# One layer of a decoder trunk: the S5 stage rewritten in chunks of 16 with one scan in a turning frame, and parameters and bias rows worked out during the projection

## The reference, cut to what matters

```python
h = rms_norm(x, g_mix); proj = h @ w_in          # (2048,1024) @ (1024,7168)
# columns: q,k,v of 3 groups x 8 heads x 64 | u: 512 channels of S5 | gate_a | gate_b
logits = einsum('nbqhd,nbkhd->nbhqk', qb, kc) + bias    # window of 128 steps, dilation 1, 4, 16
bias = bias_table[bucket]                               # by distance, per head
# S5, per group of 16 channels (32 groups), 64 complex states:
a_bar = exp(lam * dt); b_bar = ((a_bar - 1) / lam) * b_mat
# x_t = a_bar x_{t-1} + b_bar u_t ;  y_t = Re(C x_t) + D u_t   (associative scan over 2048 steps)
y_s = gelu(y)                                           # then a sigmoid gate
x = x + (sigmoid(gate_a) * (A @ W_a) + sigmoid(gate_b) * (S @ W_s)) @ w_out
x = x + moe(rms_norm(x))                                # top 4 of 32 experts
```

## Time and profile before

| | us |
|---|---|
| three runs | 5672.62, 5674.24, 5676.24 (median 5674.24) |
| the profiled execution | 5676.82 |
| its span | 5675.2 |

### The profile page before, as it was taken

The page is one execution under the profiler, slowest core; times in us unless marked ns, Lnnn a source line. Parts: engine busy times, 40 slices in busy tenths (PEclk is TensorE's granted clock), DMA queues, the critical chain, the costliest instruction groups (busy, mean ns, idle before and its releaser), DMA issues.

```text
span 5675.2 us, 81720 instructions
## 1 busy us (share of the span) xinstructions
PE 5272.8 (93%) x30128; PEld 4680.6 (82%) x30128; DVE 3105.4 (55%) x5828; ACT 1728.8 (30%) x2756; POOL 987.1 (17%) x829
## 2 busy tenths in 40 slices
PE   8999999986996997869699999999999999999997
PEld 7888888876884886758599899899989999999997
DVE  4313130006664666625455666666677777777776
ACT  4112111110102664113232333333333344444343
POOL 0000000003310200212312231313132222222221
PEclk9999999995557998989799999999999999999999
DMA  3122221210003434434345454545456666666665
GB/s 138 67 76 72 72 76 67 78 72 5 0 0 119 142 125 146 157 137 135 115 171 170 149 185 151 191 149 190 154 191 221 212 218 220 221 219 218 219 219 186
DMA packets 237535, 802.38 MB, mean 141 GB/s; under 512 B 32503, under 2 KB 52623, under 8 KB 201521
## 3 DMA queue, kind: packets, MB, share of 16 engines
q1 hardware_dynamic: 198960, 673.21, 32.1%
q0 software_dynamic: 32656, 106.62, 7.9%
q10 hardware_dynamic: 5760, 20.45, 1.1%
HBM read 652.88 MB, written 147.89 MB: 141 GB/s over the span
## 4 chain that ended last, share of the span: by engine, by line
PE 44%; DVE 4%; ACT 1%; issue 1%; DMA 0%; POOL 0%; DVEq 0%; ACTq 0%; POOLq 0%
PE ex_g L1892 27%; PE ex_d L1906 15%; DVE ex_y L2041 2%; PE ex_g L1878 1%; ACT ex_wgh L1945 1%; DVE ex_wdl L1999 1%; DVE ex_wgl L1993 1%; DVE ex_t L2020 0%; DVE ex_bgu L2014 0%; DMA ex_xg<-h_d,ex_nxt 0%; POOL ex_y L1848 0%; DMA ex_nxt<-slots_d 0%; ACT ex_xh L1958 0%; POOL out L1851 0%; DVEq L2052 0%
## 5 line engine op out<-in xcount | busy, mean ns | idle before, releaser
L1892 PE MATMUL ex_g<-ex_xh,ex_wgh 128*128 128x256 f32 (+2 forms) x4352 | 1292.3, 297 | 71.9 <-DVE ex_t L2020 64.5
L1892 PE MATMUL ex_g<-ex_xh,ex_wgl 128*128 128x256 f32 (+2 forms) x4352 | 1284.3, 295 | 0.0
L1892 PE MATMUL ex_g<-ex_xl,ex_wgh 128*128 128x256 f32 (+2 forms) x4352 | 1284.2, 295 | 0.0
L1892 PEld LDWEIGHTS ex_g<-ex_xh,ex_wgh 128*128 128x128 f32 x4352 | 823.4, 189 | 101.6 <-issue 71.1
L1892 PEld LDWEIGHTS ex_g<-ex_xl,ex_wgh 128*128 128x128 f32 x4352 | 823.8, 189 | 8.5
L1892 PEld LDWEIGHTS ex_g<-ex_xh,ex_wgl 128*128 128x128 f32 x4352 | 824.6, 189 | 0.0
L1993 DVE TENSOR_TENSOR ex_wgl<-ex_wg,ex_wgh 128x2048 fp32r<-128x2048 f32 x274 | 626.6, 2287 | 54.8 <-ACT ex_wgh L1945 52.2
L1945 ACT ACTIVATE ex_wgh<-ex_wg 128x2048 fp32r<-128x2048 f32 x274 | 524.4, 1914 | 394.2 <-PE ex_g L1892 366.8
L1848 POOL TENSOR_SCALAR ex_y<-ex_y,ex_cur 128x1024 f32<-128x1024 f32 x82 | 294.9, 3597 | 1601.2 <-DVE ex_y L2041 1601.2
L1906 PE MATMUL ex_d<-ex_wdh,ex_ath 128*128 128x512 f32 x1312 | 523.4, 399 | 0.0
L1906 PE MATMUL ex_d<-ex_wdl,ex_ath 128*128 128x512 f32 x1312 | 515.7, 393 | 0.0
(11 more groups left out here) (354 smaller groups left out, 8656.8 us busy)
## 6 DMA issues: line engine op xcount, KB each, us to landing
ex_wg<-in_w_gu SPq DMA_DIRECT2D x276, 1024.0 KB, 5.6
ex_wd<-in_w_down SPq DMA_DIRECT2D x276, 512.0 KB, 6.3
qkv_d<-prj_o SPq DMA_DIRECT2D x144, 256.0 KB
att_blk<-qkv_d SPq DMA_DIRECT2D x48, 768.0 KB, 4.2
prj_raw<-in_w_in SPq DMA_DIRECT2D x112, 256.0 KB, 3.6
ex_bd<-in_b_down SPq DMA_DIRECT2D x34, 512.0 KB
gate_d<-prj_o SPq DMA_DIRECT2D x64, 256.0 KB
mix_ring<-gate_d SPq DMA_DIRECT2D x32, 512.0 KB, 3.8
```

The lines of the kernel that those rows point to most:

```text
L1892: last = pe.matmul(gu[j][:, 0:size], w[:, k, j, :], x[:, k, 0:size], start=(k == 0 and x is xh and w is h), stop=(k == KD - 1 and w is l))
```

## The change

**S5.** Chunks of 16, so 128 of them; four batches of four pairs (`BP`, `NB`). POOL orders a batch's tokens in one copy (128x2048) and makes `inm` of a batch in six products of 128x1024, with one buffer for all batches; the output maps are now DVE's (`output_map`, six of 128x1088). PE makes only the first 16 rows of each Toeplitz matrix (`first_rows`, two products); SP copies them shifted, by 16 transfers per batch inside SBUF (`shift`). The chunk states are multiplied by a table of cosines and sines, so that the recurrence has a real factor, scanned for the whole batch by one `tensor_tensor_scan` of 128x1024, and turned back.

**Projection.** The parameters (`maps`, at m = 3) and the tables (`table`, at m = 6, stored to DRAM) are worked out on DVE, the bias rows at m = 9 (three products on PE after tile 8); at m = 10 SP writes the bias rows 128 times over to DRAM (`rep_d`), from where attention reads them already shifted and in order. `RAW` falls to 4, `RING` to 9, and seven of the eight splits of a matrix stand at t = 15.

**Attention.** `bias_tables` and `jflip` are gone; SP loads the bias per group (`load_bias`); q of the next block is turned and saved at j = 0 and not at j = 1.

The diff, cut:

```diff
-TS = 8
+TS = 16
...
-    XR, RAW, RING, OR, OB = 3, 6, 10, 3, 6
+    XR, RAW, RING, OR, OB = 3, 4, 9, 3, 6
+    MAPS, TABLES, BIAS = 3, 6, 9
...
-            return [first] if t == 5 else [first + 1] if t == 8 else list(range(first + 2, first + KD)) if t == NT - 1 else []
+            return [first] if t == 5 else list(range(first + 1, first + KD)) if t == NT - 1 else []
...
+                        if (m, t) == (BIAS, 11):
+                            store_rows()
+                        if (m, t) == (BIAS + 1, 4):
+                            sp.wait_ge(rows_out, 16 * NG)
+                            sp.dma_start(rep_d, on_rows(rows_d.rearrange("h s -> (h s)"), P)).then_inc(rep_out, 16)
...
+                        if (m, t) == (BIAS, 8):
+                            pe.wait_ge(negated, 1)
+                            for g in range(NG):
+                                if g == 2:
+                                    pe.wait_ge(rows_saved, 1)
+                                pe.matmul(pt[g % 2][0:HG, 0:STEPS_W], rel[:, g * HG:(g + 1) * HG], hot[g], start=True,
+                                          stop=True).then_inc(rows_mm, 1)
...
+                def shift(b):
+                    sp.wait_ge(d_added, b + 1)
+                    sp.wait_ge(zeroed, 1)
+                    if b >= 2:
+                        sp.wait_ge(y_mm, BP * (b - 1))
+                    for h in range(2):
+                        for j in range(JT):
+                            sp.dma_start(intra[b % 2][SC * j:SC * (j + 1), :, h, SC * j:W],
+                                         first[SC * h:SC * (h + 1), :, 0:W - SC * j]).then_inc(f_out[b % 2], 16)
+                for b in range(NB):
+                    shift(b)
+                    if b >= 2:
+                        sp.wait_ge(o_saved, 4 * (b - 1))
+                        sp.dma_start(y_out[:, b - 2, :], yT[b % 2][:, :]).then_inc(y_stored[b % 2], 16)
+                    if b + 2 < NB:
+                        load_table(b + 2)
...
+                def input_map(b):
+                    go(outer(pool, itmp[0], rr, br, b, TS))
+                    if b:
+                        pool.wait_ge(in_turned, BP * b)
+                    outer(pool, itmp[1], ri, bi, b, TS).then_inc(inm_ready, 1)
+                    pool.wait_ge(inm_ready, 3 * b + 1)
+                    go(pool.tensor_tensor(inm[:, :, 0, :], itmp[0][:, :, :], itmp[1][:, :, :], ALU.subtract))
+                    go(outer(pool, itmp[0], rr, bi, b, TS))
+                    outer(pool, itmp[1], ri, br, b, TS).then_inc(inm_ready, 1)
+                    pool.wait_ge(inm_ready, 3 * b + 2)
+                    pool.tensor_tensor(inm[:, :, 1, :], itmp[0][:, :, :], itmp[1][:, :, :], ALU.add).then_inc(inm_ready, 1)
+                    pool.wait_ge(inm_ready, 3 * b + 3)
...
+                        last = pe.matmul(ps_f[:, q % 2, :], bblk[:, p, r, :], cpad[b % 2][:, q, r, 0:W], start=(r == 0),
+                                         stop=(r == 1))
...
+                            for k in range(KT):
+                                last = pe.matmul(ps_x[q // 2][rows, q % 2, r, :], inT[p % 2][:, k, r, rows],
+                                                 u8[b % 2][:, q, h, k, :], start=(k == 0), stop=(k == KT - 1))
...
+                def outputs(b):
+                    pe.wait_ge(f_out[b % 2], 16 * 2 * JT * (b // 2 + 1))
+                    for q in range(BP):
+                            pe.matmul(out[:, h, :], u8[b % 2][:, q, h, 0, :], intra[b % 2][:, q, h, :], start=(h == 0),
+                                      stop=False)
+                            pe.matmul(out[:, h, JT * SC:], u8[b % 2][:, q, h, 1, :], intra[b % 2][:, q, h, 0:W - JT * SC],
+                                      start=False, stop=False)
+                        if q == 0:
+                            pe.wait_ge(st_ready, b + 1)
+                        for h in range(2):
+                                last = pe.matmul(ps_y[p % 2][:, h, :], st[b % 2][:, h, r, q, :],
+                                                 cpad[b % 2][:, q, r, SC:], start=False,
+                                                 stop=(h == 1 and r == 1))
+                        last.then_inc(y_mm, 1)
...
+                def output_map(b):
+                    z = b % 2
+                    if b >= 2:
+                        dve.wait_ge(y_mm, BP * (b - 1))
+                    n = W + SC
+                    outer(dve, ctmp[0], pr, cr, b, TS + 1)
+                    go(outer(dve, ctmp[1], pi, ci, b, TS + 1))
+                    go(tt(cpad[z][:, :, 0, :], ctmp[0][:, :, :], ctmp[1][:, :, :], ALU.subtract))
+                    outer(dve, ctmp[0], pi, cr, b, TS + 1)
+                    go(outer(dve, ctmp[1], pr, ci, b, TS + 1))
+                    stt(cpad[z][:, :, 1, :], ctmp[0][:, :, :], -1.0, ctmp[1][:, :, :], ALU.mult, ALU.subtract).then_inc(
+                        cpad_ready, 1)
+                    dve.wait_ge(cpad_ready, b + 1)
...
+                        dve.memset(decay[:, :, :, 0:1], 0.0)
+                    dve.wait_ge(tab_in[z], 16 * (b // 2) + 16)
+                    dve.wait_ge(x_saved, 2 * b + 2)
+                    re, im = xs[:, :, 0, :], xs[:, :, 1, :]
+                    for t, x, w in ((rt[0], re, ct), (rt[1], im, sn), (rt[2], im, ct), (rt[3], re, sn)):
+                        tt(t, x, w, ALU.mult).then_inc(rotated, 1)
+                    dve.wait_ge(rotated, 4 * b + 4)
+                    tt(z_in[:, 0, :, :], rt[0], rt[1], ALU.add)
+                    go(tt(z_in[:, 1, :, :], rt[2], rt[3], ALU.subtract))
+                    dve.tensor_tensor_scan(flat(z_out), flat(decay), flat(z_in), 0.0, ALU.mult, ALU.add).then_inc(scanned, 1)
+                    dve.wait_ge(scanned, b + 1)
+                    re, im = z_out[:, 0, :, :], z_out[:, 1, :, :]
...
+                    for n in range(4):
+                        dve.wait_ge(o_turned, 4 * b + n + 1)
+                        dve.tensor_copy(yT[b % 2][:, :].rearrange("p (n j) -> p j n", j=TS)[:, 4 * n:4 * n + 4, :],
+                                        ps_o[:, :, :]).then_inc(o_saved, 1)
...
+                def load_bias(g):
+                    heads = slice(g * HG, (g + 1) * HG)
+                    shifted = bass.AP(rep_d.tensor, rep_d.offset + g * HG * STEPS_W + P - 1,
+                                      [[len(GROUPS) * HG * STEPS_W - 1, P], [STEPS_W, HG], [1, 2 * P]])
+                    sp.dma_start(bias[:, heads, :], shifted).then_inc(bias_in[g], 16)
...
-                        if j == 1:
+                        if j == 0:
                             turn_q(n + 1)
+                    if j == 0 and blocks[n][0] != blocks[n - 1][0]:
+                        dve.wait_ge(bias_in[blocks[n][0]], 16)
```

More of the change, by code:

```diff
@@ L607, in _ @@
[L607 to L623 removed]
+                            rows = slice(SN * h, SN * (h + 1))
@@ new lines, in chunk_states, with forward @@
+                            for k in range(KT):
+                                last = pe.matmul(ps_x[q // 2][rows, q % 2, r, :], inT[p % 2][:, k, r, rows],
+                                                 u8[b % 2][:, q, h, k, :], start=(k == 0), stop=(k == KT - 1))
+                    last.then_inc(x_mm, 1)
+                def forward(b):
+                    for q in range(BP):
+                        p = b * BP + q
+                        turn_inputs(p)
+                        turn_map(p)
+                        first_rows(p)
+                        chunk_states(p)
@@ new lines, in turn_outputs @@
+                def turn_outputs(b):
+                    pe.wait_ge(y_saved, BP * b + BP)
+                    for n in range(4):
+                        if b or n:
+                            pe.wait_ge(o_saved, 4 * b + n)
+                        for j in range(4):
+                            last = pe.transpose(ps_o[:, j, :], tok[:, 4 * n + j, b * P:(b + 1) * P], ident[:, :])
+                        last.then_inc(o_turned, 1)
+                forward(0)
+                forward(1)
+                for b in range(NB):
+                    outputs(b)
+                    if b:
+                        turn_outputs(b - 1)
+                    if b + 2 < NB:
+                        forward(b + 2)
@@ L775, in bucket_onehot @@
+                dve.wait_ge(c_in, 48)
+                dve.wait_ge(eye_ready, 1)
+                output_map(0)
+                output_map(1)
+                for b in range(2):
+                    add_skip(b)
+                    scan(b)
+                for b in range(NB):
+                    if b + 2 < NB:
+                        output_map(b + 2)
+                        add_skip(b + 2)
+                        scan(b + 2)
+                    save_yT(b)
 def bucket_onehot():
@@ L847, in attention @@
-def attention(nc, qkv_d, q_gain, k_gain, bias, ident, pieces, att_d):
+def attention(nc, qkv_d, q_gain, k_gain, rep_d, ident, pieces, att_d):
     NB, PR = 6, 3
```

762 lines of the change are left out of this document (410 added, 352 removed).

## The result

The changed kernel took 5355.22 us (median of 4 runs, 5353.55 to 5358.59) and the one before 5675.24 (4 runs), a ratio of 0.9437 (95% interval 0.9421 to 0.9453). 5369 was predicted, with 5315 to 5462.

| stretch | before | after | difference | predicted |
|---|---|---|---|---|
| until S5's block begins | 1262.3 | 1269.85 | +7.5 | +7.4 |
| S5's block to attention's first instruction (before: with the bias block) | 514.0 | 216.0 | −298.0 | −295 |
| attention, to the first product of the mixing | 438.7 | 409.0 | −29.7 | −18 |
| the rest | 3460.2 | 3458.4 | −1.8 | 0 |

The account below looks back on a forecast made before the run. PE was taken to bound the projection, and S5 at half clock. S5 −295, attention −18 and projection +7.4 sum to −305.6 on 5676.8, giving 5371.2; that execution being 2.6 above the median, 5369 us, range 5315 to 5462.

Parts of the forecast that it names:

- scan(1): S5: DVE's scan of batch 1, put at 15 us beside POOL, ending 93 us after the block's start.
- The chain itself: S5: POOL, PE and DVE work in turn, block 219 us instead of 514.0, 295 us gained.
- the rival that had a chance of 0.13: S5: DVE and POOL shut each other out, overlapping maps and scans run one after the other; 5403, chance 0.13.
- The forward parts: S5: PE's transposes, first rows and chunk states of a batch; 15.6 us for four pairs, plus restart or table switch.
- the switch of table: S5: ACT's switch of table from GELU to copy, 1.3 us, charged in forward(2), forward(3) and outputs(2).
- a restart at half clock: S5: each restart of PE's list runs at most 3 us at half clock, then at full clock.
- The turning: S5: PE turns outputs and DVE copies them, alternating on one PSUM tile; 6.4 us per batch, 12.8 for batches 2 and 3.
- The scan instruction: S5: DVE's single scan instruction for a batch, taken as 1.8 us, bounded by 1.285 and twice that.
- Shifts: S5: 16 small transfers per batch, about 6 us with issues, hidden under the 13 us scan on DVE.
- Attention: Attention: −20 for q turned one step earlier (bounds −37 and 0), +2 for group 0's bias load; sum −18 us.
- Projection: Projection: bias rows +2.4, start +2, changes of matrix +3, parameters and tables hidden; sum +7.4 us.
- the low-clock rival: S5: PE's clock stays at 1.2 GHz, +85 us after taking off 12 for restarts already counted; 5454, chance 0.17.

Follow-up runs that it names:

- pool_halves: The changed kernel with each of POOL's products of 1024 columns cut in two of 512; 5356.76 us, ratio 0.9447.
- kept_busy: The changed kernel with turns of the identity on PE in the places where it waits in S5; 5349.72 us, ratio 0.9427.
- maps_early: The changed kernel with a second PSUM tile for turned outputs and POOL's input maps made in the projection, loaded by S5 from DRAM; 5307.31 us, ratio 0.9352.
- order_back: The changed kernel with q of the next attention block turned and saved at j = 1 again; 5383.56 us, ratio 0.9492.
- order_alone: The kernel before with only q of the next attention block turned and saved at j = 0; 5645.94 us, ratio 0.9951.

## Why the prediction was right, and where its parts were not

The removal of PE's long list was right, and so was the order of the new chain; that the sum came so near is in part luck, as the table shows. The time of each point on the chain, counted from the block's start:

| end of | predicted | measured |
|---|---|---|
| POOL's map 0 | 28 | 23.3 |
| forward(0) | 47 | 40.4 |
| forward(1) | 77.6 | 64.2 |
| scan(1) | 93 | 89.1 |
| output_map(2) | 101.5 | 96.9 |
| forward(2) | 118.4 | 111.0 |
| scan(2) | 133.4 | 131.2 |
| output_map(3) | 148.1 | 147.1 |
| forward(3) | 165 | 160.1 |
| outputs(3) | 199.1 | 191.9 |
| last turning | 211.9 | 208.8 |
| block | 219 | 216.0 |

Step by step, those that took longer than predicted (scan(1) 9.5 us, scan(2) 5.2, the last turning 4.1, the turning of batch 0 with output_map(3) 1.2) make 20 us, those that took less 23. Neither alone would have left the range: without the ones the time would have been some 5335, without the others some 5378 (estimates from these rows).

- **The chain itself was right**: from batch 1 on, POOL's map, forward parts, scans and output maps followed one another as predicted, with PE waiting where it was said to (15.5 and 7.1 us for output maps 2 and 3, where some 8 each was said). What was not foreseen is that forward(0) waited 2.7 us for DVE's first output map, which took 15.2 us beside POOL and not 8.2.
- **DVE beside POOL was undersized, POOL oversized.** From the small instructions of before I read factors, 1.2 and 1.46. They need not have been factors: POOL's instructions of S5 were 0.2 to 0.75 us long there, so that a wait for a whole one was short; no run tests this on the old stage, but it fits. With 1.9 us each, DVE's 0.6 became 2.4. The scans of batches 0, 1 and 2 took 27.6, 21 and 20.4 us, not 15. It was the mechanism of the rival that had a chance of 0.13, yet at the time of the forecast and not at that rival's 5403; this is the luck in it. The Trainium skill ("SBUF — State Buffer", "Who interferes with whom") says that the one that issues first has the shared ports for its whole instruction and the other blocks, and that a DVE instruction with two SBUF inputs does not contend with one that only writes SBUF; the waits above, their halving in pool_halves (1.84 to 0.91 us) and the memset beside which DVE ran at 1.28 us agree with both. What kept the sum: POOL's product took 1.93 us alone, less than the 2.39 of the nearest row, so its map took 15.5 us and not 18; the ordering 1.9 and not 3.2; and the longest scan, that of batch 0, lay beside forward(1).
- **The forward parts were oversized**: 13.0 to 14.3 us from PE's last wait (the first pair's turning, some 1 us, lay before it in three of them), not 16.9 to 18.6. A pair at full clock is 3.08 us (3.9 predicted; ACT's copies lay beside PE), and the switch of table that was charged twice there and once in outputs(2) did not occur: one load in all of S5 where L634 alone had seven before. The sum charged 3 us for a restart at half clock in forward(0) and forward(1) and nothing in the other two, though the text says at each. Two of them can be read: forward(2) took 14.1 us from its first row and 11.3 in kept_busy, so 2.8 us; forward(3) 13.0 and 11.3, so 1.7. The half clock lasted longer than the "at most 3 us" of the text (0.50 in 1366 to 1372, 0.95 in 1372 to 1380), and the price of 2.8 us is about half of that stretch. The rival (clock low through S5) did not come: 0.94 and 1.00 in the windows above.
- **The turning was undersized**: 6.4 us for four groups were 7.7 at batch 0, the last eight 16.9 and not 12.8, as PE ran at half clock between its waits and alternated with DVE.
- **The scan instruction** took 2.29 us, inside the bounds (1.3 to 2.6), above the 1.8 chosen. Shifts: 10.3 us to issue and 2.3 to land, not 6; hidden from outputs, as predicted. What the prediction did not name is that they also hold `first`: those of batch 0 had landed only some 2 us before ACT's next copy into it (1326.9), and in maps_early this wait came out.
- **Attention was undersized**: −29.7, not −18, inside −37 to 0. The price was chosen by the products' waits (19.1 us); the weight loads' waits (36.8 before, 2.4 after) stood nearer. And the 2 us put down for the bias tile's first load did not come (order_back, order_alone).
- **Projection**: +7.5 for +7.4, in one pair of executions; over the seven with this projection it was +6.0 to +7.5. Its start was +2.9 (predicted 2; 1.9 to 3.7 over the seven), the bias rows some 2.2, a wait of 0.7 among them (2.4 predicted), so that 2.4 are left for the changes of matrix (3 predicted; what is left over, not measured there), and nothing for the maps and tables: DVE's busy time in 133 to 912 rose from 210.8 to 272.5 us with PE at 779.00.
- **Sums that do not come out**: the low-clock rival takes off 12 us "for restarts already counted", but the sum holds 6, so its cost was +91 and not +85. The bounds −12 and +10 for POOL's products count 21 of them, while the chain as written has 11 on it, −7 and +6.

So S5's block came out 3 us shorter than predicted, with errors of both signs inside it that nearly cancelled, and attention's gain 12 us larger, which is most of the 14 us between 5369 and 5355.

## What to carry to other kernels

Read contention of DVE and POOL as a wait for the other's whole instruction, not as a factor: what was 20% beside short instructions is a factor of four beside 2 us ones, and the cure is to put POOL's work where DVE is idle, not to cut it up. When a stage stops being bound by one engine, look at single tiles that make two engines alternate, and at gaps that put TensorE back to 1.2 GHz: here they were worth 16 and 8 us. Price a wait on TensorE's path by its weight loads' wait, which came 48 times where that of the products came 26: here 36.8 us of the one foretold a gain of 27.5 to 29 us in attention's time, and 19.1 of the other did not.
